# Sample-attention scores of a hybrid decoder step: 32x32 tiles of the array and block-turned key pages

## The reference, cut to what matters

```python
logits = jnp.einsum('btgrd,btkgd->btgrk', qg, k_sel, preferred_element_type=F32) * (D ** -0.5)
logits = logits + jnp.transpose(bias, (0, 1, 3, 4, 2))
logits = jnp.where(valid[:, :, None, None, :], logits, -1e30)
p = jax.nn.softmax(logits, axis=-1)
o = jnp.einsum('btgrk,btkgd->btgrd', p.astype(v_sel.dtype), v_sel)
```

## Time and profile before

| | us |
|---|---|
| median of 3 runs | 2083.68 (2083.51 to 2085.29) |
| the profiled execution's own time | 2083.23 |
| its span, first to last instruction | 2081.6 |
| TensorE busy | 2066.7 (99%) |
| VectorE busy | 1291.4 (62%) |
| ScalarE busy | 736.1 (35%) |
| GpSimd busy | 409.7 (20%) |
| mean granted TensorE clock, share of full speed | 0.997 |

### The profile page before, as it was taken

The page is one execution under the profiler, slowest core; times in us unless marked ns, Lnnn a source line. Parts: engine busy times, 40 slices in busy tenths (PEclk is TensorE's granted clock), DMA queues, the critical chain, the costliest instruction groups (busy, mean ns, idle before and its releaser), DMA issues. The chain is left out here.

```text
span 2081.6 us, 38868 instructions
## 1 busy us (share of the span) xinstructions
PE 2066.7 (99%) x14183; PEld 1974.2 (95%) x14183; DVE 1291.4 (62%) x1747; ACT 736.1 (35%) x917; POOL 409.7 (20%) x574
## 2 busy tenths in 40 slices
PE   9999999999999999999999999999999999999998
PEld 7888888999999999999999999999999999999998
DVE  5545545578687445656786767565565866655664
ACT  6433333322222333333333323333334433333333
POOL 1100000021220010235642103222222511111100
PEclk9999999999999999999999999999999999999999
DMA  8777777755554565665666657878777855555554
GB/s 235 209 219 213 222 211 204 213 165 159 157 160 140 178 192 171 176 198 172 194 201 202 179 153 231 242 246 260 247 246 248 258 170 169 164 163 166 156 167 147
DMA packets 341330, 406.03 MB, mean 195 GB/s; under 512 B 20332, under 2 KB 316204, under 8 KB 341000
## 3 DMA queue, kind: packets, MB, share of 16 engines
q1 hardware_dynamic: 293704, 291.75, 47.7%
q0 software_dynamic: 29968, 94.61, 14.5%
q10 hardware_dynamic: 17584, 18.70, 2.7%
HBM read 377.68 MB, written 31.45 MB: 197 GB/s over the span
## 5 line engine op out<-in xcount | busy, mean ns | idle before, releaser
L246 DVE TENSOR_TENSOR lo<-raw,hi 128x1024 fp32r<-128x1024 f32 x542 | 697.3, 1290 | 564.1 <-ACT hi L241 562.7
L270 PE MATMUL main<-XX,hi 128*128 128x320 f32 x3264 | 1029.4, 315 | 0.2 <-DVE XX L1652 0.2
L272 PE MATMUL main<-XX,lo 128*128 128x320 f32 x3264 | 1008.8, 309 | 0.0
L271 PE MATMUL main<-XX,hi 128*128 128x320 f32 x3264 | 1008.3, 309 | 0.0
L241 ACT ACTIVATE hi<-raw 128x1024 fp32r<-128x1024 f32 x542 | 570.6, 1059 | 853.4 <-PE main L272 541.0
L270 PEld LDWEIGHTS main<-XX,hi 128*128 128x128 f32 x3264 | 613.1, 188 | 9.1 <-issue 5.0
L271 PEld LDWEIGHTS main<-XX,hi 128*128 128x128 f32 x3264 | 613.2, 188 | 2.3
L272 PEld LDWEIGHTS main<-XX,lo 128*128 128x128 f32 x3264 | 612.7, 188 | 0.0
L257 PE MATMUL main<-XX,hi 128*128 128x512 f32 x1024 | 355.9, 392 | 0.0
L258 PE MATMUL main<-XX,lo 128*128 128x256 f32 x1024 | 286.8, 280 | 0.0
L257 PEld LDWEIGHTS main<-XX,hi 128*128 128x128 f32 x1024 | 191.5, 187 | 42.5 <-issue 0.2
(11 more groups left out here) (304 smaller groups left out, 1548.0 us busy)
## 6 DMA issues: line engine op xcount, KB each, us to landing
raw<-w_in SPq DMA_DIRECT2D x416, 512.0 KB, 3.9
raw<-w_out SPq DMA_DIRECT2D x128, 512.0 KB, 3.7
deck<-cache_k POOLq DMA_DIRECT2D x64, 256.0 KB, 4.2
projT<-stg ACTq DMA_DIRECT2D x35, 320.0 KB, 2.9
keep<-cache_v POOLq DMA_DIRECT2D x40, 256.0 KB, 3.6
deck<-cache_v POOLq DMA_DIRECT2D x24, 256.0 KB, 3.8
deck<-maskD POOLq DMA_DIRECT2D x8, 516.0 KB, 5.7
ipg<-cache_idx_k POOLq DMA_DIRECT2D x64, 64.0 KB, 3.1
```

What stands on the lines that cost most here:

```text
L246: nc.vector.tensor_tensor(low, raw[:, slot, :, 0:width], high.bitcast(F32), ALU.subtract).then_inc(lo_ready, 1)
L270: nc.tensor.matmul(sums, wh, XH[:, k, :], start=first, stop=False)
L271: nc.tensor.matmul(sums, wh, XL[:, k, :], start=False, stop=False)
L272: mm = nc.tensor.matmul(sums, wl, XH[:, k, :], start=False, stop=last)
```

## The change

The key transposes on TensorE go. VectorE turns a whole page at once in blocks of 32x32 (one `nc.vector.transpose` of 128 x 512 a page) into `KX`, whose rows then hold position within a block and whose blocks are spread over four slots. The scores are formed by 64 products of 32 rows, 32 columns of weights and 256 columns in the 16 tiles of the array, plus 4 small ones for the new keys. The queries must lie on the lanes that match, so ScalarE makes four shifted copies of them (`qB`, 11 small copies a row). VectorE reads the scores out of four banks with five instructions for one. The turns of a row's pages are spread over VectorE's steps of the row before: for row 2q+1 in steps 5, 6 and 7 of the quad, for row 2q+2 in steps 13, 14 and step 0 of the next quad; for row 0 in steps 0, 1, 2 of the first quad. GpSimd's order of loads changes.

```diff
             def pe_weave(pe, q, j):
-                if s in (1, 2):
-                    for p in range(4 * s - 4, 4 * s):
...
-                        for g in range(G):
-                            tr = nc.tensor.transpose(sbank[p % 4][:, g * P:(g + 1) * P], kpg[:, p, g * P:(g + 1) * P], ident[:])
-                        tr.then_inc(e_kt, 1)
                 if s == 3:
...
-                    for c in range(0, LS, 512):
-                        z = min(LS, c + 512)
-                        for g in range(G):
-                            mm = nc.tensor.matmul(wide[32 * g:32 * g + 32, c:z], qb[:, 32 * g:32 * g + 32], KTs[:, g, c:z],
-                                                  start=True, stop=True, skip_group_check=True)
+                    pe.wait_ge(e_ptA, b)
+                    pe.wait_ge(e_o, b)
+                    pe.wait_ge(e_kn, b + 1)
+                    pe.wait_ge(e_kt, b * PAGES + PAGES)
+                    pe.wait_ge(e_qB, b * COPIES + COPIES)
+                    alone(pe)
+                    for c in range(4):
+                        for a in range(4):
+                            for g in range(G):
+                                rows, quarter = slice(32 * a, 32 * a + 32), slice(32 * g, 32 * g + 32)
+                                nc.tensor.matmul(sbank[a][quarter, 0:PAST // 4], qB[rows, (c - a) % 4, quarter],
+                                                 KX[rows, 4 * g + c, :, :].rearrange("p n k -> p (n k)"),
+                                                 start=c == 0, stop=c == 3, skip_group_check=True)
+                    for g in range(G):
+                        quarter = slice(32 * g, 32 * g + 32)
+                        mm = nc.tensor.matmul(sbank[0][quarter, PAST // 4:PAST // 4 + T_S], qB[:, 0, quarter], KN[:, g, :],
+                                              start=True, stop=True, skip_group_check=True)
                     mm.then_inc(e_s, 1)
...
+            def turned_pages(dve, b, pages):
+
+                for p in pages:
+                    if p == 0:
+                        dve.wait_ge(e_k, b * (16 * PAGES) + 16 * PAGES)
+                        if not isinstance(b, int) or b > 0:
+                            dve.wait_ge(e_s, b)
+                        dve.wait_ge(w_pe, 4 * NG)
+                        dve.wait_ge(ut_out, 16 * NG * (NB_S + 1))
+                    nc.vector.transpose(KX[:, :, p, :], kpg[:, p, :].rearrange("p (b k) -> p b k", k=32)).then_inc(e_kt, 1)
...
+            SPREAD = [(0, 0, 4)] + [(d, a, n) for d, n in ((2, 2), (1, 1), (3, 1)) for a in range(0, 4, n)]
...
+                for d, a, n in SPREAD[slice(*QPART[part])]:
+                    c = (a + d) % 4
+                    nc.scalar.activation(qB[32 * a:32 * (a + n), d, :].rearrange("p (h n) -> p h n", h=H),
+                                         qS[32 * c:32 * (c + n), :, ds(b * T_S, T_S)], ACT.Copy).then_inc(e_qB, 1)
...
+            TURNS = {5: (1, range(0, 2)), 6: (1, range(2, 5)), 7: (1, range(5, PAGES)),
+                     13: (2, range(0, 3)), 14: (2, range(3, 6)), 0: (0, range(6, PAGES))}
+            FIRST = (range(0, 3), range(3, 6), range(6, PAGES))
+
+            def dve_weave(dve, q, j, first=False, last=False):
...
+                if first and j < 3:
+                    if j == 0:
+                        new_keys(dve, 0)
+                    turned_pages(dve, 0, FIRST[j])
+                elif j in TURNS and not (last and j > 8):
+                    ahead_, pages = TURNS[j]
+                    turned_pages(dve, q * BQ + ahead_, pages)
...
-                    nc.vector.scalar_tensor_tensor(lgS, wide[:, 0:LS], SCALE, lgS, ALU.mult, ALU.add).then_inc(e_lg, 1)
+                    for a in range(4):
+                        logits = lgS[:, 0:PAST].rearrange("p (n a k) -> p a n k", a=4, k=32)[:, a]
+                        nc.vector.scalar_tensor_tensor(logits, sbank[a][:, 0:PAST // 4].rearrange("p (n k) -> p n k", k=32), SCALE,
+                                                       logits, ALU.mult, ALU.add)
+                    nc.vector.scalar_tensor_tensor(lgS[:, PAST:LS], wide[:, PAST // 4:PAST // 4 + T_S], SCALE, lgS[:, PAST:LS],
+                                                   ALU.mult, ALU.add).then_inc(e_lg, 1)
...
-                load_pages(pool, 0, "cache_v", vpg, e_v, 3)
+                load_pages(pool, 0, "cache_v", vpg, e_v, 3, 5)
+                pool.wait_ge(e_kt, PAGES // 2)
+                load_pages(pool, 1, "cache_k", keys, e_k, 0, PAGES // 2)
+                load_pages(pool, 0, "cache_v", vpg, e_v, 5)
                 load_vnew(0)
-                with pool.Fori(1, NB_S) as b:
-                    pool.wait_ge(e_kt, b * PAGES)
-                    alone(pool)
-                    load_pages(pool, b, "cache_k", keys, e_k)
+                pool.wait_ge(e_kt, PAGES)
+                load_pages(pool, 1, "cache_k", keys, e_k, PAGES // 2)
+
+                def load_row(b, more):
                     pool.wait_ge(e_pt, b)
                     alone(pool)
                     load_mask(b)
+                    if more:
+                        pool.wait_ge(e_kt, b * PAGES + PAGES)
+                        alone(pool)
+                        load_pages(pool, b + 1, "cache_k", keys, e_k)
                     pool.wait_ge(e_pv, b)
                     alone(pool)
                     load_pages(pool, b, "cache_v", vpg, e_v)
                     load_vnew(b)
+                with pool.Fori(1, NB_S - 1) as b:
+                    load_row(b, True)
+                load_row(NB_S - 1, False)
```

More of the change, by code:

```diff
@@ L155, in hybrid_layer @@
         ptab = sb("ptab", [1, NB_S * PAGES], I32)
-        keep = sb("keep", [P, G * N + (LS + 1) // 2 + L2 + L2 // 2 + 3 * KVW + POOLW // P * NB_S * STATE])
+        keep = sb("keep", [P, G * N + 4 * H * T_S + L2 + L2 // 2 + 3 * KVW + POOLW // P * NB_S * STATE])
         at = [0]
@@ L168, in hybrid_layer @@
         kT = cut(G * N).rearrange("p (g n) -> p g n", g=G)
-        maskS = cut((LS + 1) // 2, BF16)
+        qB = cut(4 * H * T_S).rearrange("p (c n) -> p c n", c=4)
         era = at[0]
@@ L178, in hybrid_layer @@
         qS = cut(H * N_S, back=era).rearrange("p (h n) -> p h n", h=H)
-        stood = {e: sem(f"stood_{e}") for e in ("Pool", "DVE", "SP", "PE")}
+        stood = {e: sem(f"stood_{e}") for e in ("Pool", "DVE", "SP", "PE", "Activation")}
         def alone(eng):
@@ L1373, in last_stage @@
             rel = deal(LS)
-            KTs = deal(G * LS).rearrange("p (g n) -> p g n", g=G)
+            KX = deal(G * PAST).rearrange("p (b n k) -> p b n k", n=PAGES, k=32)
+            KN = deal(G * T_S).rearrange("p (g n) -> p g n", g=G)
             free = after_qS + KEPT * KVW
-            qb = keep[:, free:free + P]
-            oN = keep[:, free + P:free + P + HD]
+            oN = keep[:, free:free + HD]
             st1 = sb("st1", [P, 4], ctx=ph)
@@ L1419, in pe_weave @@
-                if s == 3:
-                    pe.wait_ge(e_kcA, b * (PAGES // 2) + PAGES // 2)
-                    pe.wait_ge(e_kcD, b * (PAGES // 2) + PAGES // 2)
-                    pe.wait_ge(e_kn, b * 2 + 2)
-                    for c in range(0, LS, 512):
-                        z = min(LS, c + 512)
-                        for g in range(G):
-                            mm = nc.tensor.matmul(wide[32 * g:32 * g + 32, c:z], qb[:, 32 * g:32 * g + 32], KTs[:, g, c:z],
-                                                  start=True, stop=True, skip_group_check=True)
+                if s == 3:
+                    if u == 0:
+                        pe.wait_ge(a_lg, H)
+                        pe.wait_ge(a_ptc, H)
+                        pe.wait_ge(a_oh, H)
+                        pe.wait_ge(w_ev, 4 * NG)
+                        pe.wait_ge(ut_c, NG)
+                    pe.wait_ge(e_ptA, b)
[15 more added lines that the diff above has]
+                                              start=True, stop=True, skip_group_check=True)
@@ L1449, in pe_weave @@
                     nc.tensor.transpose(sbank[3][:, P:2 * P], oN, ident[:]).then_inc(e_ot, 1)
[L1451 to L1458, removed]
@@ new lines, in new_keys, with spread_queries @@
+            def new_keys(dve, b):
+                if isinstance(b, int) and b == 0:
+                    dve.wait_ge(w_pe, 4 * NG)
+                else:
+                    dve.wait_ge(e_s, b)
+                nc.vector.tensor_copy(KN, kT[:, :, ds(b * T_S + T_P, T_S)]).then_inc(e_kn, 1)
+            SPREAD = [(0, 0, 4)] + [(d, a, n) for d, n in ((2, 2), (1, 1), (3, 1)) for a in range(0, 4, n)]
+            COPIES = len(SPREAD)
+            QPART = ((0, 3), (3, 7), (7, COPIES))
+            def spread_queries(act, b, part):
+                if part == 0:
+                    act.wait_ge(e_in, 16)
+                    if isinstance(b, int) and b == 0:
+                        act.wait_ge(w_pe, 4 * NG)
+                    else:
+                        act.wait_ge(e_s, b)
+                    alone(act)
```

(36 more changed lines are left out.)

18 lines of the change are left out of this document (2 added, 16 removed).

## The result

The change makes the kernel slower: 2109.28 us, median of 4 runs (2105.86 to 2110.63), beside 2083.60 of the kernel before; ratio 1.012 (95% interval 1.0108 to 1.0132). Forecast were 2094 and a range up to 2108. The profiled execution took 2110.63 us, its span is 2109.1.

A forecast was written before the change was run, and what follows sets the result against it. It took TensorE's own work to bound the stage. First quad -0.5 plus 3 x (2.2 for value waits + 1.8 for the clock) made +11.5 us on 2083.2, 2094.7; it predicted 2094, range 2082 to 2108.

The forecast's parts named there:

- It just fits: Odd row's value block: values landed at U + 27.0 to 27.8, needed at U + 28.2, so no wait.
- The value pages: GpSimd issues keys before values; TensorE idles 8.4 us ahead of the value block in rows 2, 4, 6.
- The score block: TensorE's scores in 16 tiles take 2.4 us against 2.1, +0.3 us a row.
- bounds of 2.2 and 4.0: Score block: 2.2 us is column time and old overhead; 4.0 us if passes start 28 ns apart.
- the 16 tiles are not what they say: Rival, chance 0.18: score block of 4.0 us gives 2102; row strips one after another give 2119.
- a 7.3: Upper bound in us for the score block, if the four row strips run one after another.
- The clock: After each long TensorE pause, 3.6 us at 1.2 GHz, a loss of 1.8 us; bounds 0 and 3.6.
- Values late, clock kept: Rival, chance 0.17: same waits at the value block, no clock loss; 2086, between 2082 and 2088.
- Row 0: First quad: TensorE waits 4.0 us for VectorE's turns of row 0's key pages before scoring.
- The turns: VectorE's block transposes of 128x512, eight a row: 0.65 us each, bounds 0.5 and 0.87.
- The wait at the boundary: At each quad start TensorE waits 0.25 us for VectorE's split of chunk 3.
- the values are in time: Rival, chance 0.15: no wait at the value block, TensorE's saved work alone counts; 2063.

The follow-up runs named there:

- before_longer: The kernel before with its four small score products issued nine more times, 144 more TensorE instructions a quad; 2095.25 us, ratio 1.0055.
- half_products: values_first with 32 score products a row for 64, half of the contraction left out; 2059.93 us, one run.
- unrolled: values_first with TensorE's loop over quads 0 to 2 written out, same work; 2070.63 us, ratio 0.9938 against the kernel before.
- all_three: values_first with unrolled's edit and row 0's key pages turned earlier; 2066.71 us, ratio 0.9918 against the kernel before.
- values_first: The changed kernel with GpSimd issuing row b's values before the keys of row b+1; 2076.63 us, ratio 0.9969 against the kernel before.
- half_cols: values_first with score products taking 128 columns for 256, the scores of key pages 4 to 7 left out; 2071.94 us, one run.

## Why the prediction was wrong in size and right in kind

The sign, the mechanism and its place came out as forecast; the time lies 15 us above it and 1 us above the range. I set the stage's forecast of +11.5 us against what the profiled executions show: 2110.6 - 2083.2 = +27.4, of which 26.8 in the stage and 0.7 ahead of it. What failed is two terms of the sum, the score block's 2.4 us and the instruction fetches that it put at nothing, and the step "It just fits". By its steps:

- **The value pages, the forecast mechanism: right.** TensorE stood ahead of the value block in rows 2, 4 and 6 for 8.7, 8.4 and 9.4 us (forecast 8.4 each). Keys were free earlier than I said (first key page at T + 11.5, not 13.5), the issues took longer (20.4 us, not 18.8), the landing too (6.2, not 4.5): T + 38.1 in place of 36.8. TensorE was there at T + 29.4, not 28.4. That the wait came out so close to 8.4 is partly luck: -2.0, +1.6, +1.7 and -1.0 cancel. The step **"It just fits"** failed: the odd row waited 2.4 us in row 3 and 0.8 in row 5. Its first key page came at U + 4.4, as forecast (4.5), but the issues took 21.3 and 19.8 us for 18.8 and the landing 6.0 and 5.8, so the values were there at U + 31.7 and U + 30.0, not at 27.0 to 27.8. All five waits: 29.8 us, 4.6 over the 25.2 forecast.
- **The score block: mis-sized.** "I take 2.4" was 3.07 in the trace; 0.66 more in 8 rows is 5.3 us. (By the prediction's own rule a shorter block would only have lengthened the wait in the five rows that waited for values, so three rows, 2.0 us, lie on the path; no run of the change's order tests this.) The bounds of 2.2 and 4.0 held it. My sum had the columns right, since halving them took just their time away, and the overhead wrong: 1.35 us against 0.7. Of the rival "the 16 tiles are not what they say" nothing is left: the tiles do run side by side, a 7.3 is ruled out, and starts come closer than 28 ns. The Trainium skill, "TensorE: Matmul & The Clock Gate", section "Wait — 56ns, not 53.3ns?", would have no starts nearer than about 25 ns; my estimate from it is a block of 3.2 us and more for 128 passes. Here 128 take 2.76, 22 ns each, and in before_longer 72 take 0.63, so the measurement decides against it where passes go to different tiles.
- **Instruction fetches: missing altogether.** No term of the sum has them. TensorE's work on a row grew by 80 records (136 of scores for 24 and the 32 key transposes), its loop's body by 160, and the body no longer stays fetched, as I read the packets and the stops; seven stops in the stage make 7.1 us from start to start, 6.1 more than seven normal steps. half_products, unrolled and before_longer show the cause from three sides. The prediction counted what instructions cost in time and not that they are instructions.
- **The clock: right.** At the row 0 pause and at each of three 8 to 9 us pauses the clock fell to 0.50. From the value block to chunk 8 the even rows took 7.3, 8.0 and 7.9 us for 5.89, so 1.4, 2.1 and 2.0 lost; with 2.4 at row 0 (from score block to value block 16.98 us, for 14.61 in row 2 of all_three) that is 7.9, forecast 4 x 1.8 = 7.2. The pause of 2.4 us in row 3 left no such stretch. "Values late, clock kept" falls with it.
- **Row 0: right.** 4.0 us forecast (1327.0 + 3.52 is 1330.5, so its own figures give 4.2), 3.7 measured. **The turns: right**, 0.68 us each for 0.65. **The wait at the boundary** of 0.25 us didn't come: the fetch stops at the quad's end give VectorE that time.

That starts could come closer than 28 ns, the trace of the kernel before already showed, and I misread it: the 28 ns of the earlier trace rows are a mean. These are its value block's first 40 ns and the 70 after them (us; busy time of PE and of PEld, the weight loads; PEclk, DMA share, GB/s):

```profile
1422.26:1422.30 0.04, 0.03 (x4) 0.03 (x5) 1.00 0.76 206
1422.30:1422.37 0.07, 0.07 (x4) 0.07 (x8) 1.00 0.73 133
```

Four passes, one to a column strip, start within 40 ns, and no other in the next 70, so 28 ns is no distance that all starts keep.

Summed: 4.6 + 5.3 + 6.1 + 0.7 - 0.3 - 0.75 = 15.7, where 27.4 - 11.5 = 15.9 us were missing, or 15.3 in the stage alone. The rival "the values are in time", given 2063, is what values_first built. Its profiled execution took 2078.6, some 16 us more: the block's 0.66 x 8 = 5.3, the fetches' 8.7 (seven stops, 9.7 us less seven steps of 0.147) and the clock's 2.7, less 1.3 that row 0 and the boundaries fell short of forecast, make 15.4. My words that it would need a chain 8.4 us shorter saw only the chain's length and not that its order could be turned.

What stays open: what sets the 16-tile block's pace. After the first 32 passes, which start 6 to 7 ns apart with one stop of 0.14 us between, most follow at about 17 ns, whatever the order, with stops of up to 0.2 us; short passes over four column strips go at 8.8. Each pass brings a weight load, and no run keeps the passes and drops the loads, so whether these set the pace is not shown. Also open is why the loop written out still has a fetch stop or two (0.8 us in unrolled, 1.3 in all_three, start to start).

## What to carry to other kernels

When a change merges two loads into one burst on an in-order queue, write down for each load who waits for it and by when, and issue first what is due first: here the order cost 33 us, more than the 28 that the removed transposes had taken. Count instructions as well as time: a loop body that stays fetched in one form may not in the next, and the profile's page shows it in the instruction queue's packets together with waits on "issue". Written out the loop cost nothing here and gave 6 us.

## What the runs showed of the hardware that I had not expected

- TensorE's loop body of the kernel before, and one of 32 records more (half_products), stays fetched; one of 144 or 160 records more (before_longer, the change) does not: 64 packets for 44, with stops of 0.6 to 2.1 us (start to start; the longest in half_cols) at two or three places of the loop. Written out (unrolled) it has 59 packets and one stop of 0.8 us. Where between 32 and 144 it turns I didn't look for.
- Passes in 16 different tiles start 6 to 7 ns apart at first and mostly 17 ns apart later; 8-column passes over four column strips follow at 8.8 ns.
- A 16 KB load behind sixteen 256 KB pages landed 5.6 us after its issue in the median, and 3.6 in values_first, where keys and values are apart.
- In this stage every stop of TensorE of 3.8 us and more, from start to start, was followed by a granted clock of 0.50, in every run. Of the shorter ones, one of 1.95 us was too (values_first); one of 2.50 (the change, row 3) and one of 2.08 us (half_cols) were not.
